# Sample decode in a hybrid decoder step: twelve value tiles in one accumulation, placed ahead of the second head's transposes

## What is computed

```python
# A: forgetting attention over 1024 cached keys (8 pages of 128) and the sample's own key
s = q.k * SCALE + (c_q - c_k);  oa = softmax(s) @ v
# B: dilated attention; windows (128,1), (512,4), (2048,16), mixed by their softmax denominators
o_p = (ex_p / l_p) @ v_p;  lse_p = m_p + log(l_p);  ob = sum_p softmax(lse)_p * o_p
out = concat(oa, ob) @ w_out
```

## Time and profile before

| | |
|---|---|
| median of 3 executions | 2758.29 us (2755.62 to 2760.85) |
| the profiled execution | 2759.74 us |
| its span in the trace | 2757.9 us |
| attention stage in the trace | 425 to 778 us |
| mean granted TensorE clock over the span | 0.98 of full |
| TensorE matmuls busy | 2631.2 us (95%) |
| VectorE, ScalarE, GpSimd busy | 1161.8, 543.9, 1121.1 us |

### The profile page before, as it was taken

How to read it: one execution, slowest core, us unless ns; L and a number is a source line. 1 busy time by engine, 2 the same in 40 slices (tenths; PEclk the granted TensorE clock), 3 DMA queues, 4 the chain that set the end, 5 groups by cost and what they waited for, 6 DMA issues and landing times.

```text
span 2757.9 us, 43275 instructions
## 1 busy us (share of the span) xinstructions
PE 2631.2 (95%) x16553; PEld 2402.2 (87%) x16553; DVE 1161.8 (42%) x2274; ACT 543.9 (20%) x1263; POOL 1121.1 (41%) x726
## 2 busy tenths in 40 slices
PE   5899988989999999999999998998999999999999
PEld 3787765556689999999999996898999999999999
DVE  4763735656615433333333343144453333333333
ACT  3210106555622100000000033312210000000001
POOL 4423214454575444444443345414464444333330
PEclk8999999999999999999999999999999999999999
DMA  4222226656620211111111111111021111111101
GB/s 116 60 76 85 76 64 190 191 185 193 186 79 16 70 47 46 46 46 46 49 49 46 46 38 35 43 32 47 16 62 47 47 49 49 46 46 49 50 31 62
DMA packets 220766, 189.88 MB, mean 69 GB/s; under 512 B 29571, under 2 KB 173443, under 8 KB 220644
## 3 DMA queue, kind: packets, MB, share of 16 engines
q1 hardware_dynamic: 202084, 163.99, 20.4%
q10 hardware_dynamic: 18560, 24.25, 2.5%
HBM read 171.19 MB, written 17.01 MB: 68 GB/s over the span
## 4 chain that ended last, share of the span: by engine, by line
PE 64%; DVE 4%; POOL 1%; ACT 1%; issue 1%; ACTq 0%; POOLq 0%; DVEq 0%
PE ps L489 61%; DVE hs L448 1%; PE ps L521 1%; PE ps L523 1%; PE ps L522 1%; POOL acc_sq L416 1%; ACT ps L1806 1%; DVE Xl L1881 0%; POOL Xl L462 0%; DVE Xl L462 0%; DVE acc_sq L440 0%; PE ps L1781 0%; POOL Wl L378 0%; PE ps L1918 0%; DVE VM_EARLY L1871 0%
## 5 line engine op out<-in xcount | busy, mean ns | idle before, releaser
L489 PE MATMUL ps<-Xh,Wh 128*128 128x256 f32 (+2 forms) x2712 | 875.6, 323 | 15.3 <-DVE Xl L1881 6.5
L489 PE MATMUL ps<-Xl,Wh 128*128 128x256 f32 (+2 forms) x2712 | 869.6, 321 | 0.0
L489 PE MATMUL ps<-Xh,Wl 128*128 128x256 f32 (+2 forms) x2712 | 868.5, 320 | 0.0
L364 POOL TENSOR_TENSOR Wh<-raw,zeros 128x1024 fp32r<-128x1024 f32 x185 | 367.1, 1984 | 1136.0 <-PE ps L489 790.0
L489 PEld LDWEIGHTS ps<-Xh,Wh 128*128 128x128 f32 x2712 | 512.4, 189 | 20.6 <-issue 8.6
L489 PEld LDWEIGHTS ps<-Xl,Wh 128*128 128x128 f32 x2712 | 512.5, 189 | 1.0 <-issue 0.3
L489 PEld LDWEIGHTS ps<-Xh,Wl 128*128 128x128 f32 x2712 | 512.8, 189 | 0.0
L367 POOL TENSOR_TENSOR Wl<-raw,Wh 128x1024 fp32r<-128x1024 f32 x185 | 455.9, 2464 | 14.5
L1597 DVE TENSOR_TENSOR Hl<-hf,Hh 128x392 fp32r<-128x392 f32 (+1 forms) x132 | 181.3, 1373 | 464.7 <-ACT Hh L1525 464.7
L489 PE MATMUL ps<-Hh,Wh 128*128 128x392 f32 (+2 forms) x1056 | 341.5, 323 | 2.4 <-DVE xT L1606 2.3
L489 PE MATMUL ps<-Hl,Wh 128*128 128x392 f32 (+2 forms) x1056 | 338.7, 321 | 0.0
(11 more groups left out here) (201 smaller groups left out, 2530.3 us busy)
## 6 DMA issues: line engine op xcount, KB each, us to landing
raw<-in_w_gate_up SPq DMA_DIRECT2D x88, 512.0 KB, 3.8
raw<-in_w_down SPq DMA_DIRECT2D x44, 512.0 KB, 3.5
kring<-in_cache_a_k SPq DMA_DIRECT2D x64, 256.0 KB, 3.7
ring<-in_cache_a_v SPq DMA_DIRECT2D x64, 256.0 KB, 3.3
raw<-in_w_in_even SPq DMA_DIRECT2D x25, 512.0 KB, 4.2
raw<-in_w_in_c SPq DMA_DIRECT2D x16, 512.0 KB, 3.8
xs<-in_x_prompt SPq DMA_DIRECT2D x8, 512.0 KB, 4.6
q_prompt<-zt ACTq DMA_DIRECT2D x16, 256.0 KB, 2.0
```

Source lines behind the costliest of these rows:

```text
L364: pool.tensor_tensor(h[:, :], r[:, :], zeros[:, :].to_broadcast([P, 1024]), ALU.add).then_inc(split_high, 1)
L489: ins = nc.tensor.matmul(out, w, x, start=(j == 0), stop=(j == len(pairs) - 1))
```

## The change

Exponentials of B now go to columns 8 to 15 of `Lp`, and those of A stay in columns 0 to 7. So all twelve tiles may accumulate into the same rows of bank 7: the rows of a column group hold A's eight heads and then B's eight. One mask, one scale (`wl_`) and one gather then serve both; the gather multiplies by two columns of `hmask` that tell A's rows from B's. ScalarE takes the exponentials in two instructions rather than one. The burst moves from behind `transpose_weights(u + 1, 1)` to ahead of it, and waits for all eleven loaded tiles.

```diff
-        TURN_AT, SPREAD_AT, SUM_AT, PAGES_AT, DILATED_AT = 6, 7, 8, 8, 9
+        TURN_AT, SPREAD_AT, SUM_AT, VALUES_AT = 6, 7, 8, 8
 ...
             def load_values(it, tiles):
                 for j in tiles:
-                    positive_wait(sp, page_ps if j < PAGES else dil_ps, it)
+                    positive_wait(sp, values_ps, it)
 ...
-                    for g in range(2):
-                        for i in range(4):
-                            last = nc.tensor.matmul(ps[i * LW:(i + 1) * LW, 6, 3 * P + g:3 * P + g + 1], Ls[:, g, :], ones[:, 0:1],
-                                                    start=True, stop=True)
-                if sample_at(u, PAGES_AT + 2) is not None:
-                    pe.wait_ge(dch, DCH * sample_at(u, PAGES_AT + 2) + 10)
-                    last = gather(sample_at(u, PAGES_AT + 2), 0)
-                if sample_at(u, DILATED_AT + 2) is not None:
-                    pe.wait_ge(osamp, 2 * sample_at(u, DILATED_AT + 2) + 1)
-                    last = gather(sample_at(u, DILATED_AT + 2), 1)
+                    for i in range(4):
+                        last = nc.tensor.matmul(ps[i * LW:(i + 1) * LW, 6, 3 * P:3 * P + 1], Ls[:, :], ones[:, 0:1], start=True, stop=True)
+                if sample_at(u, VALUES_AT + 2) is not None:
+                    last = gather(sample_at(u, VALUES_AT + 2))
 ...
-            def sample_values(it, tiles, done):
+            def sample_values(it):
                 pe.wait_ge(dp_done, it + 1)
-                for j in tiles:
-                    if ring_slot(j) is not None:
-                        pe.wait_ge(ring_in[ring_slot(j)], 16 * (it + 1))
+                for j in VALUE_ORDER:
+                    pe.wait_ge(ring_in[ring_slot(j)], 16 * (it + 1))
                 if it == 0:
                     pe.wait_ge(own_in, 32)
-                for n, j in enumerate(tiles):
-                    rows = slice(LW * (n % 4), LW * (n % 4) + LW)
-                    last = nc.tensor.matmul(ps[rows, 7, :], Lp[:, j, :], value_tile(j), start=(n < 4), stop=(n + 4 >= len(tiles)))
-                last.then_inc(done, 1)
+                for j in range(LOG):
+                    rows = slice(LW * (j % 4), LW * (j % 4) + LW)
+                    last = nc.tensor.matmul(ps[rows, 7, :], Lp[:, j, :], value_tile(j), start=(j < 4), stop=(j + 4 >= LOG))
+                last.then_inc(values_ps, 1)
 ...
-                transpose_weights(u + 1, 1)
-                pages, dilated = (sample_at(u, at) for at in (PAGES_AT, DILATED_AT))
-                if pages is not None or dilated is not None:
+                sample = sample_at(u, VALUES_AT)
+                if sample is not None:
                     sample_bank_free(u)
                     pe.wait_ge(qk_act, qk_jobs_before(u + 1, 0))
                     pe.wait_ge(qk_dve, qk_jobs_before(u + 1, 1))
-                if pages is not None:
-                    sample_values(pages, list(range(PAGES + 1)), page_ps)
-                if dilated is not None:
-                    sample_values(dilated, list(range(PAGES + 1, LOG)), dil_ps)
+                    sample_values(sample)
+                transpose_weights(u + 1, 1)
 ...
-                    act.activation(Lp[:, :, 0:HEADS], Lb[:, :, :], ACT.Exp).then_inc(dp_done, 1)
+                    act.activation(Lp[:, 0:PAGES + 1, 0:HEADS], Lb[:, 0:PAGES + 1, :], ACT.Exp)
+                    act.activation(Lp[:, PAGES + 1:LOG, HEADS:2 * HEADS], Lb[:, PAGES + 1:LOG, :], ACT.Exp).then_inc(dp_done, 1)
```

More of the change, by code:

```diff
@@ L788, in build @@
         dist_in = sems("dist_in", 3)
-        page_ps, dil_ps, dmask, lp_zero, own_zero = (sem(n) for n in ("page_ps", "dil_ps", "dmask", "lp_zero", "own_zero"))
+        values_ps, dmask, lp_zero, own_zero = (sem(n) for n in ("values_ps", "dmask", "lp_zero", "own_zero"))
         PAIRS = 8
@@ L1046, in window @@
                 positive_wait(pe, o_out, u)
-                if sample_at(u, DILATED_AT + 3) is not None:
-                    pe.wait_ge(osamp, 2 * sample_at(u, DILATED_AT + 3) + 2)
+                if sample_at(u, VALUES_AT + 3) is not None:
+                    pe.wait_ge(osamp, sample_at(u, VALUES_AT + 3) + 1)
                 it, qt = unit(u)
@@ L1077, in window, with gather @@
                 last.then_inc(pv_ps, 1)
-            def gather(it, g):
-                pe.wait_ge(dmask, 2 * it + g + 1)
+            def gather(it):
+                pe.wait_ge(dmask, it + 1)
                 for c in range(4):
-                    last = nc.tensor.matmul(ps[:, 6, 3 * P + 8 + c:3 * P + 9 + c], MV[0:MROWS[g], c * P:(c + 1) * P],
-                                            ones[0:MROWS[g], 0:1],
-                                            start=True, stop=True)
+                    last = nc.tensor.matmul(ps[:, 6, 3 * P + 2 * c:3 * P + 2 * c + 2], MV[:, c * P:(c + 1) * P],
+                                            hmask[:, HEADS:HEADS + 2], start=True, stop=True)
@@ L1281, in sample_sums, with sample_mask, gathered @@
                 dve.wait_ge(dp_done, it + 1)
[L1282 to L1287, removed]
+                step(dve.tensor_reduce(Ls[:, 0:HEADS], Lp[:, 0:PAGES + 1, 0:HEADS].rearrange("p j h -> p h j"), AX, ALU.add))
+                step(dve.tensor_reduce(Ls[:, HEADS:2 * HEADS], Lp[:, PAGES + 1:LOG, HEADS:2 * HEADS].rearrange("p j h -> p h j"), AX, ALU.add))
+            def sample_mask(it, u):
+                dve.wait_ge(values_ps, it + 1)
                 dve.wait_ge(dch, DCH * it + 10)
                 dve.wait_ge(pv_ps, u)
[L1290 to L1293, removed]
-            def gathered(it, g, w):
+                dve.scalar_tensor_tensor(MV[:, :].rearrange("p (h e) -> p h e", h=HEADS),
+                                         ps[:, 7, :].rearrange("p (h e) -> p h e", h=HEADS), wl_[:, 0:1],
+                                         hmask[:, 0:HEADS].unsqueeze(2).to_broadcast([P, HEADS, HD]), ALU.mult, ALU.mult).then_inc(dmask, 1)
+            def gathered(it, w):
                 dve.wait_ge(pv_ps, w + 1)
-                dve.tensor_copy(oS[:, 4 * g:4 * g + 4, it], ps[:, 6, 3 * P + 8:3 * P + 12]).then_inc(osamp, 1)
+                dve.tensor_copy(oS[:, :, it].rearrange("p (g c) -> p g c", g=2),
+                                ps[:, 6, 3 * P:3 * P + 8].rearrange("p (c g) -> p g c", g=2)).then_inc(osamp, 1)
             def after_window(w):
@@ L1308, in after_window @@
                     dve.wait_ge(pv_ps, w + 1)
-                    step(dve.reciprocal(wl_[:, :], ps[:, 6, 3 * P:3 * P + 2]))
-                if sample_at(w, PAGES_AT + 2) is not None:
-                    gathered(sample_at(w, PAGES_AT + 2), 0, w)
-                if sample_at(w, DILATED_AT + 2) is not None:
-                    gathered(sample_at(w, DILATED_AT + 2), 1, w)
+                    step(dve.reciprocal(wl_[:, :], ps[:, 6, 3 * P:3 * P + 1]))
+                if sample_at(w, VALUES_AT + 2) is not None:
+                    gathered(sample_at(w, VALUES_AT + 2), w)
             for g in (1, 3):
@@ L1322, in att_dve @@
                     after_window(u)
-                if sample_at(u - 1, PAGES_AT) is not None:
-                    sample_mask(sample_at(u - 1, PAGES_AT), 0, u + 1)
-                if sample_at(u - 1, DILATED_AT) is not None:
-                    sample_mask(sample_at(u - 1, DILATED_AT), 1, u + 1)
+                if sample_at(u - 1, VALUES_AT) is not None:
+                    sample_mask(sample_at(u - 1, VALUES_AT), u + 1)
                 if u >= 0 and QK_AT.get(j) in (1, 3) and it < PAIRS - 1:
@@ L2177, in shape_constants @@
     db[P // 2:, :, 3, :] = np.where(mine[:P // 2], np.log(3.0), NEG)[:, :, None]
-    hmask = (np.arange(P)[:, None] % 32 == np.arange(HEADS)[None, :]).astype(f)
+    row = np.arange(P)[:, None] % 32
+    hmask = np.concatenate([(row % HEADS == np.arange(HEADS)[None, :]) & (row < 2 * HEADS), row // HEADS == np.arange(2)[None, :]], 1).astype(f)
     return {"c_ident": np.eye(P, dtype=f), "c_uo": np.concatenate([tri, np.ones((P, SEQ - P), f)], 1),
```

21 lines of the change are left out of this document (10 added, 11 removed).

## The result

The changed kernel takes **2783.6 us** (median of 4 runs, 2781.2 to 2784.4); the kernel before, run beside it, 2759.6 (4 runs, 2755.6 to 2761.0). The ratio is **1.0086, 95% interval 1.0070 to 1.0102**: 24 us slower. The forecast was 2775, range 2762 to 2788, slower with a chance of 0.8. The profiled execution took 2783.8 us with a span of 2782.0.

A forecast was written before the change was run, and what follows sets the result against it. TensorE was taken to set the pace of the attention stage, with tile 11's issue and landing deciding the case. The sum -17 + 24 + 9 = +16 us gave 2775 us, range 2762 to 2788.

The forecast's parts named there:

- What goes, 17 us: TensorE's attention stage: second bursts, second gathers, mask waits, four sums and sample 7 save 6.9 + 4.6 + 2.9 + 0.8 + 0.7 + 1.0.
- sample 7's 1.0: Last sample, before the output projection: GpSimd's work moves up with unit 62's output, counted as 1.0 us saved.
- the 2.9 that were counted: `transpose_qk`'s waits for the second mask in U+2, four of seven places, go: 2.9 of 5.0 us saved.
- The two gathers called hidden: Second gathers of sample 0 (unit 14) and sample 3 (unit 35): said to save nothing; five others save 4.6 us.
- the rival of their price: Burst's three added tiles don't share the third turn: 8 x 0.99 come back, +24 us, 2783; chance 0.07.
- The waits, 24 us: TensorE's burst waits for tile 11 in samples 0, 1, 2, 4, 5 and 6, landing 4.2 us after issue: 24 us.
- The reason for samples 4 and 5: Short units: SP issues without a break, so tile 11 goes late; new waits of 7.7 and 5.2 us.
- The clock, 9 us: TensorE falls to half rate after long stalls: three drops of 3.0 us, 9 us, bounded by two and six, 6 to 18.
- The tile is there in time: Rival at the burst: tile 11 lands before TensorE comes, only savings count, -17 us, 2742; chance 0.10.
- No drop: Rival on TensorE's clock: no drop follows the stalls, 24 - 17 = +7 us, 2766; chance 0.15.
- stalls fall where TensorE waits anyway: Rival at units 15, 23, 31: bias load runs ahead during stalls of samples 0 to 2, +5 us, 2764; chance 0.13.
- Every stall is dearer: Rival on the stalls: six drops rather than three, +25 us, 2784, or 2789 with landings near 5 us; chance 0.10.

The follow-up runs named there:

- experiment 3: The changed kernel with value loads issued three a unit instead of two, so tile 11 goes two units earlier: 2756.4 us, 0.9973.
- experiment 4: The changed kernel with only the last value load, tile 11, moved ahead of its unit's key loads in SP's queue: 2769.4 us, 1.0026.
- Experiment 6: The changed kernel with unused matmuls (7, 7 and 5) run ahead of the burst's waits of samples 4, 5 and 6: 2777.4 us, 1.0058.
- experiment 11: The changed kernel with loads three a unit, burst in U+1 and dilation tiles waited for before the third turn: 2743.0 us, 0.9934.
- the loads alone: The kernel before, with its two bursts, and value loads issued three a unit: 2755.2 us, 0.9979.
- experiment 5: The changed kernel with tiles 9 to 11 waited for only before the third turn of matmuls, order unchanged: 2763.8 us, 1.0003.
- experiment 9: The changed kernel with value loads three a unit and the merged burst one unit later, in U+1: 2747.3 us, 0.9942.

## Why the prediction held, and where it didn't

**What goes, 17 us: right in size.** Without sample 7's 1.0 it was 16.0. The three units behind each burst are shorter by 14.7 us in sum for the samples 0 to 6, and another 1.6 us of unit 54 is there but turns into a wait for sums (unit 55). `transpose_qk`'s wait for the mask went from 5.0 to 2.1 us, the 2.9 that were counted, and in U+2 it doesn't wait. The two gathers called hidden were hidden: unit 14 and unit 35 lost one each, and the next wait for sums grew by as much. The gathers are half as many: 64 matmuls in a busy time of 9.3 us instead of 128 in 17.7. The burst of twelve takes 2.7 us at full clock (sample 2), so three more tiles are free, and the rival of their price is out. Sample 7 gave less than its 1.0: from the start of unit 60 to the output projection it takes 17.3 us against 17.6. GpSimd's work does move up with unit 62's output, as said; the projection comes 6.6 us behind that output in both kernels.

**The waits, 24 us: right, 25.3.** The total wait was put at 27.7 us and is 28.7. Sample by sample it was less good: 3.45, 3.53, 1.16, 7.42, 7.97, 5.16 against 3.9, 2.2, 2.1, 8.8, 6.8, 3.9. Landings of tile 11 spread from 3.2 to 5.3 us around the 4.2 taken; that the total came out so close is in part luck, as the errors of the six have both signs. The constant part of about 2.0 us that the Trainium skill gives (page "DMA: Bandwidth & Descriptors", fixed cost) is below every one of them; the row was the better price.

**The reason for samples 4 and 5: incomplete.** The prediction said that "SP itself is late: it issues without a break". It is, but experiments 3 and 4 show a second limit: in the short units the DMA engines are near full, and sample 4's tile, 4.0 us in landing, took 5.4 when it was put ahead of the keys and 6.2 when it was issued 6.6 us sooner in its unit. The first landed no sooner for it, the second 4.5 us. The number came out right since the landing was read from the loaded queue; a fix built on the reason as given misses, and experiment 3's did, by 16 us, some of it for this. The limit stood in the kernel before, where the stretch of sample 4's first burst and of tile 11's issue has a DMA share of 0.91:

```profile
652.00:660.00 8.00, 6.95 (x86) 4.25 (x85) 3.19 (x13) 3.75 (x8) 4.56 (x6) 1.00 0.91 291
```

For samples 0, 1 and 2 the reason held (experiment 4); for 6 it was the smaller part: issued 2.7 us sooner its tile landed 0.6 sooner.

**The clock, 9 us: mis-sized, 13.7.** "Three drops" at 3.0 us each; there were five bursts with a lengthened rest, each 1.0 to 3.1 us, and a further drop of 3.2 in unit 55. Sample 0's wait of 3.45 us, called "near" unit 23's 4.56, and sample 1's 3.53 did halve the rate. So the count of three was too low, six would have been right, and 3.0 us a drop is the upper end of what they cost, 2.3 on average. The drop behind the wait of 1.63 us in unit 55 had no place in the sum at all. Experiment 6 shows that it is the clock: with the stalls filled the rate holds and some 10 us come back. The Trainium skill's warning (page "TensorE: Matmul & The Clock Gate", on oscillation) went the right way: five of the six stalls have a clock of 0.50 behind them.

**Given back, about 5 us: missing.** The prediction let only two hidden gathers be lost at later waits for sums. That wait grew by 7.0 us. 1.8 of them are those gathers, at units 15 and 39; the rest, 5.2, is mostly at units 31 (2.65), 55 (1.63) and 15 (another 1.2). The timeline of the changed kernel, units 15 and 31, which waited 2.62 and 2.13 us before:

```profile
510.10 0.70 PE L1039 MATMUL ps<-ident,rl 128*64 128x128 f32 x4 [4.71 <-DVE rl L1221]
...
608.92 0.69 PE L1039 MATMUL ps<-ident,rl 128*64 128x128 f32 x4 [4.78 <-DVE rl L1221]
```

They wait for VectorE, and VectorE waits at unit 15 for the bias load, at unit 31 for another one, of the tile `dist`:

```profile
508.54 0.75 DVE L1213 CUSTOM_DVE_ANT_0 S<-ps,bias,mx_tail 128x512 f32<-128x512 f32 x1 [3.95 <-DMA bias<-c_dram]
...
607.36 0.75 DVE L1213 CUSTOM_DVE_ANT_0 S<-ps,dist,mx_tail 128x512 f32<-128x512 f32 x1 [3.97 <-DMA dist<-in_c_dist]
```

Both are issued at the same distance from the start of the unit before as in the kernel before, 0.5 us, but land later: the bias load takes 6.0 us instead of 4.8, the `dist` load 6.1 instead of 3.8. What slows them isn't shown.

**The sum: right, with luck.** With 25.3 for 24, 13.7 for 9 and the 5 us given back the stage grew by 28.1 us, not by 16. The span grew by 24.1 only since the stage began 1.3 us earlier and the rest of the program was 2.7 us shorter, which no term forecast.

**The rivals.** "The tile is there in time", 2742, isn't this kernel, but experiment 11 is that case made: 2743. Its 16 us don't all come from the merge, though: the loads alone brought 5.8. So the merge, with its burst a unit later and waiting late, is worth some 10 us (16.0 less 5.8, from two jobs), less than 17, which fits what is given back. "No drop" and "stalls fall where TensorE waits anyway" are out by the table above; the first would have left +14 of the +28, and the second has it wrong besides that unit 31 waits for a bias load: it is the `dist` load. "Every stall is dearer", six drops, 2784, is nearest the measured time, and its count is the measured one: six drops. But they cost less than 3.0 us each, landings took 4.4 us on average rather than 4.2, and the 5 us given back, which it doesn't have either, make up for it.

**Left open.** Why the rest of the program was 2.7 us shorter, and what slowed the two loads of units 15 and 31.

## What to carry to other kernels

Merging two steps that use late data moves the deadline of the last tile to come: set its issue plus its landing, read from loads in that very stretch, against the time at which TensorE will now want it, and look at the DMA share there before counting on an earlier issue. Wait for each tile as late as the order of the matmuls allows, and let the burst stand where the tiles are in; here that, with the loads three a unit, turned +24 us into -16. On an engine that sets the pace, price a stall at its length plus the half rate behind it, and expect a part of what is saved to be lost at the next wait for something that the engine doesn't drive.

## What the runs showed of the hardware

Where the 16 DMA engines were at a share of 0.9 to 1.1 (279 to 307 GB/s) a tile that was issued sooner took longer to land, and gained only a part of it. Sample 4's 128 KB took 4.0 us behind two key loads, and 5.4 us ahead of them, so that 1.4 us of earlier issue brought nothing; it took 6.2 us when issued 6.6 us earlier in its unit, which brought 4.5. A wait of 3.45 us had a granted clock of 0.50 behind it; the 0.58 us that stood in its place in experiment 5 had none. Shorter waits had it too: 1.63 us in unit 55 of the changed kernel and 1.76 us in experiment 9 (0.56), while behind the 1.57 us of the kernel before the burst took its 1.92 us at full rate. The price of one such drop was between 1.0 and 3.2 us.
